# One-hot tables for the gate scatter: the order of VectorE's work in the one-hot part of a streaming-encoder block

## The reference

```
s1, s2  = scores of each token against two sets of 128 keys, per head (8 heads)
i1, i2  = top 16 of each; the best 16 of the 16 x 16 sums give the experts e = e1 * 128 + e2
gates   = softmax(best 16 scores)
a       = einsum("td,thkd->thk", x, u[e])         # dot with the expert's row of u
y       = einsum("thk,thkd->td", gates * gelu(a), v[e])
```

## Time and profile before

| | |
|---|---|
| median of 3 runs | 3572.12 us |
| profiled execution, its own time | 3572.59 us |
| its span | 3570.8 us |
| mean granted clock of TensorE, share of full | 0.95 |
| TensorE busy | 3241.3 us (91%) |
| VectorE busy | 2623.8 us (73%) |
| ScalarE busy | 1100.5 us (31%) |
| GpSimd busy | 653.5 us (18%) |
| moved by DMA | 883.48 MB, mean 247 GB/s |

### The profile page before, as it was taken

One profiled execution on the slowest core, in us unless ns is written; L12 is line 12 of the kernel. 1 busy time (PEld: TensorE's weight loads), 2 busy tenths in 40 slices (PEclk: granted clock), 3 DMA queues, 4 the chain that ended last, 5 costly groups with the idle time before them and its releaser, 6 DMA issues.

```text
span 3570.8 us, 46376 instructions
## 1 busy us (share of the span) xinstructions
PE 3241.3 (91%) x17301; PEld 2956.9 (83%) x17301; DVE 2623.8 (73%) x3074; ACT 1100.5 (31%) x1015; POOL 653.5 (18%) x428
## 2 busy tenths in 40 slices
PE   1598878879979899999999999999999998999999
PEld 0386764537757799999998898889999998999999
DVE  6868986865563388888877777774777777777777
ACT  2123124432122344444323223332333332233332
POOL 0200000000020002222102211220433333233333
PEclk7599989979979999999999999999999999999999
DMA  8572221125524437777647777777999998999997
GB/s 351 218 282 94 85 77 65 74 82 203 203 89 164 155 139 287 277 270 282 236 182 280 276 290 306 285 287 273 353 349 348 343 349 308 359 348 350 342 348 288
DMA packets 241085, 883.48 MB, mean 247 GB/s; under 512 B 17680, under 2 KB 132496, under 8 KB 169744
## 3 DMA queue, kind: packets, MB, share of 16 engines
q1 hardware_dynamic: 161552, 545.82, 41.2%
q0 software_dynamic: 55296, 268.46, 20.0%
q10 hardware_dynamic: 24192, 68.64, 5.1%
HBM read 824.13 MB, written 58.72 MB: 247 GB/s over the span
## 4 chain that ended last, share of the span: by engine, by line
PE 63%; DVE 20%; DMA 6%; issue 5%; ACT 4%; DVEq 1%; SPq 0%; POOL 0%; ACTq 0%; PEldq 0%
PE bank L1595 9%; PE bank L1596 9%; PE bank L1597 9%; PE bank L1294 9%; PE bank L1295 8%; PE bank L1296 8%; DVE u_row L1125 3%; ACT w_hi L430 3%; DVE tap_a L893 2%; DMA w_raw<-wwq 2%; DVE tap_b L893 2%; DMA ada_w<-wada 2%; DVE w_lo L761 2%; PE bank L1486 2%; PE bank L1487 2%
## 5 line engine op out<-in xcount | busy, mean ns | idle before, releaser
L761 DVE TENSOR_TENSOR w_lo<-w_raw,w_hi 128x2048 fp32r<-128x2048 f32 (+1 forms) x327 | 742.5, 2271 | 760.6 <-ACT w_hi L430 748.5
L1294 PE MATMUL bank<-act_hi,w_hi 128*128 128x384 f32 (+1 forms) x2840 | 1034.6, 364 | 177.8 <-POOL act_lo L402 105.6
L430 ACT ACTIVATE w_hi<-w_raw 128x2048 fp32r<-128x2048 f32 (+1 forms) x327 | 621.6, 1901 | 1517.3 <-PE bank L1296 795.8
L1295 PE MATMUL bank<-act_lo,w_hi 128*128 128x384 f32 (+1 forms) x2840 | 1017.7, 358 | 0.0
L1296 PE MATMUL bank<-act_hi,w_lo 128*128 128x384 f32 (+1 forms) x2840 | 1016.6, 358 | 0.0
L1294 PEld LDWEIGHTS bank<-act_hi,w_hi 128*128 128x128 f32 x2840 | 550.1, 194 | 245.9 <-issue 139.5
L1595 PE MATMUL bank<-wt_hi,w_hi 128*128 128x384 f32 x2048 | 688.7, 336 | 17.3 <-DVEq L1255 9.2
L1597 PE MATMUL bank<-wt_hi,w_lo 128*128 128x384 f32 x2048 | 686.7, 335 | 0.0
L1596 PE MATMUL bank<-wt_lo,w_hi 128*128 128x384 f32 x2048 | 686.6, 335 | 0.0
L1296 PEld LDWEIGHTS bank<-act_hi,w_lo 128*128 128x128 f32 x2840 | 549.3, 193 | 34.7
L1295 PEld LDWEIGHTS bank<-act_lo,w_hi 128*128 128x128 f32 x2840 | 551.3, 194 | 30.1 <-issue 0.2
(11 more groups left out here) (232 smaller groups left out, 2596.5 us busy)
## 6 DMA issues: line engine op xcount, KB each, us to landing
w_raw<-u SPq DMA_DIRECT2D x128, 1024.0 KB
w_raw<-v SPq DMA_DIRECT2D x128, 1024.0 KB
ada_w<-wada SPq DMA_DIRECT2D x80, 1024.0 KB, 5.4
gelu_l<-gelu_scratch SPq DMA_DIRECT2D x64, 768.0 KB
gate_l<-gate_scratch SPq DMA_DIRECT2D x64, 768.0 KB
w_raw<-win SPq DMA_DIRECT2D x27, 1024.0 KB
gelu_scratch<-gelu_s ACTq DMA_DIRECT2D x128, 192.0 KB
gate_scratch<-g_chunk ACTq DMA_DIRECT2D x8, 3072.0 KB, 12.4
```

The lines of the kernel that those rows point to most:

```text
L430: act.activation(w_hi[n0 % 2][:, 0:width], w_raw[n0 % 2][:, 0:width], ACT.Copy).then_inc(hi_done, 1)
L761: dve.tensor_tensor(w_lo[s][:, 0:width], w_raw[s][:, 0:width], w_hi[s][:, 0:width].bitcast(F32), ALU.subtract).then_inc(lo_done, 1)
L1294: pe.matmul(out, wh, hi_t(k), start=(k == 0), stop=False)
L1295: pe.matmul(out, wh, lo_t(k), start=False, stop=False)
```

## The change

The five instructions that build a group of one-hots become a function `build_hots(u, i)`. The group for turn 0, u = 0 is built ahead of VectorE's loop. In the loop, which now has 23 turns, VectorE makes the low half of a job, then builds the group that TensorE needs after the job that comes next (u = 1 of the same turn behind the first low half, u = 0 of the following turn behind the second), and takes the dots after that. The 24th turn is written out behind the loop. TensorE's, ScalarE's, GpSimd's and SP's programs are the same.

```diff
-            with dve.Fori(0, 24) as i:
+            def build_hots(u, i):
+
+                dve.wait_ge(hot_used[2 * u + 1], LEAD + i)
+                tok = bass.ds(i * 16 + 8 * u, 8)
+                one = T_.mark(dve.tensor_tensor(hot1[2][:, u], iotas, of_tokens(e1_c, tok), ALU.is_equal))
+                dve.tensor_tensor(hot2[:, u], iotas, of_tokens(e2_c, tok), ALU.is_equal)
+                T_.after(one)
+                for j in range(3):
+                    ins = dve.tensor_tensor(hot1[j][:, u], hot1[2][:, u], of_tokens(gate_c[j], tok), ALU.mult)
+                ins.then_inc(hot_ready[u], 1)
+
+            build_hots(0, 0)
+            with dve.Fori(0, 23) as i:
                 T_.open(i, 2)
                 for u in range(2):
-                    dve.wait_ge(hot_used[2 * u + 1], LEAD + i)
-                    tok = bass.ds(i * 16 + 8 * u, 8)
-                    one = T_.mark(dve.tensor_tensor(hot1[2][:, u], iotas, of_tokens(e1_c, tok), ALU.is_equal))
-                    dve.tensor_tensor(hot2[:, u], iotas, of_tokens(e2_c, tok), ALU.is_equal)
-                    T_.after(one)
-                    for j in range(3):
-                        ins = dve.tensor_tensor(hot1[j][:, u], hot1[2][:, u], of_tokens(gate_c[j], tok), ALU.mult)
-                    ins.then_inc(hot_ready[u], 1)
                     lo(J_U + 74 + u, i)
+                    build_hots(1 - u, i + u)
                     for m in range(1 + u):
                         dot(54 + u + m, i, 3)
-                T_.close(24)
+                T_.close(23)
+            lo(J_U + 120)
+            build_hots(1, 23)
+            dot(123)
+            lo(J_U + 121)
+            for m in range(2):
+                dot(124 + m)
```

## The result

| | median | lowest to highest | runs |
|---|---|---|---|
| before | 3572.03 us | 3570.91 to 3573.41 | 4 |
| after | 3494.23 us | 3492.39 to 3495.50 | 4 |

What follows compares the result with a forecast made beforehand. TensorE was taken to be held up each turn by VectorE's two dots ahead of the u = 0 one-hots. Waits of 52 and clock 25.4 made 77.4 us off 3572.59, about 3495 us, range 3487 to 3517.

Steps and rivals of the forecast that it cites:

- The bound: One-hot part: an 11.9 us chain from the u = 1 job outlasts TensorE's 9.77, making it 2.28 us late each turn.
- The group of u = 0: VectorE's loop: two 2.21 us dots leave the chain; one-hots done at 7.50, slack 2.3 us instead of a 2.28 wait.
- The group of u = 1: VectorE's loop: now behind two dots and the low half, done at 17.27, wanted at 19.54; the moved cost stays hidden.
- The sum: First to last group: 536.62 us becomes 459.2, gaining 77.4: 52 for the waits and 25.4 for the clock.
- The rows' side: Clock in the one-hot part: one of two turns waited without a drop, so the clock term is 25.4, not 37.
- a drop behind each wait: The skill's reading for TensorE's one-hot waits: 23 drops of 1.6 us, giving 52 + 37 = 89.
- The transfers: One-hot part: same bytes in a shorter turn, 331 GB/s instead of 285; rows and loads of u costed at nothing.
- Rival 1: One-hot store turns: late rows or loads stall VectorE's one-hots, 31 us given back in 8 turns, 3526; chance 12%.
- Rivals 2 and 3: One-hot part: 2, transfers at 285 GB/s set pace, 3572, 3%; 3, dots waiting for rows block low halves, 3620, 4%.

Runs made afterwards that it cites:

- The experiment with waits of 1.1 us: Changed kernel with one u = 1 dot and two further, overwritten one-hot instructions ahead of the u = 0 group: 3523.08 us, ratio 0.9863.
- waits are of 3.3 us: Changed kernel with both u = 1 dots and two further, overwritten one-hot instructions ahead of the u = 0 group: 3614.80 us, ratio 1.0118.
- 2 MB a turn more: Changed kernel with 2 MB more copied HBM to HBM on SP's queue in each one-hot turn: 3527.19 us, ratio 0.9873.
- 1 MB more: Changed kernel with 1 MB more copied HBM to HBM on SP's queue in each one-hot turn: 3495.01 us, ratio 0.9785.

## Why the prediction was right

**The bound.** The reading that TensorE is held up in each turn by a chain it starts itself, rounding, low half, two dots, one-hots, is shown from three sides: the dots put back bring back the time, one dot alone costs nothing, and short dots in the old order give the time of the change.

**The group of u = 0.** Forecast from the end of the u = 1 job: low half at 2.15, one-hots from 4.36 to 7.50, wanted at 9.77. In the turn from 2076.54 they stand at 2.14, 4.35 and 7.36 (2078.68, 2080.89, 2083.90), and TensorE takes them at 9.78. The five one-hot instructions take 3.01 us behind a low half, where I had taken 3.14 from behind a dot.

**The group of u = 1.** Forecast: low half at 11.92, one-hots 14.13 to 17.27, dot to 19.48, next low half at 21.7. Found: 11.93, 14.14 to 17.15, to 19.36, 21.70. TensorE takes this group at 19.56, so the slack of 2.3 us is there. (VectorE's idle time of 2.26 us before the last low half is another thing: it is what is left of its own turn.) The runs added that this slack is not used: with the dot in front, which leaves next to none, the time is the same.

**The sum.** 459.2 us from first to last group was forecast, 459.66 measured; 77.4 us of gain, 77.8 measured between the medians. I had split it in 52 for the waits and 25.4 for the clock. That split rested on two turns and a rounded 0.95, and the whole trace of the kernel before bears it out: TensorE takes the group of u = 0 2.26 us late in each of the 23 turns, and seven of the turns last 21.8 us and sixteen 23.4, that is 1.6 more, so 52 and 25. The clock falls behind 16 of 23 waits, never elsewhere in the part. The experiment with waits of 1.1 us supports it: there the lateness alone is paid, 1.22 us a turn for 1.1 shown, and the clock is untouched. The rows' side was the right one to take against a drop behind each wait: that would have given 89. The case on the page (the Trainium skill, TensorE: Matmul & The Clock Gate, "HAM oscillation") has waits of 3 to 5 us, and it was I who carried it over to 2.1. Where the waits are of 3.3 us the trace agrees with it: the clock falls in or behind each of the 23.

**The transfers.** Costed at nothing, and they cost nothing. The share of 0.85 and 330 GB/s are as forecast (0.87 and 331). The room was about as narrow as I had made it out: I gave the loads of u 15.3 us and between 0 and 2.3 us of lateness; behind two of the stores a load took 15.6 us, and the two roundings were late by 0.4. For the rows I counted on a landing of 14.81 us as the worst and 1.3 us to spare; the largest was 14.5, and the closest row landed 2.2 us before its dot. The median of 7.5 that I held against it was that of the faster kind of row, and the second row of u = 1 takes 10.6; this changes no term of the sum. Rival 1, with 12%, asked for a stall in each of 8 store turns; it takes 2 MB a turn more to bring eight such stalls about, and the rows' landing at 15.4 in the median. The mechanism exists, then, and is bound to the stores as I had it, but a dot that waits 1.3 us for its row, as with 1 MB more, still does not reach TensorE: the slack of 2.3 us lies between. By the rule cited for it (the Trainium skill, DMA: Bandwidth & Descriptors, "Issuing engines are not separate DMA queues") the transfers interleave: a copy on SP's queue made the rows of GpSimd's queue slower, 15.4 us for 9.9 with all rows counted in both, so the trace agrees.

**Rivals 2 and 3.** 285 GB/s was no ceiling: the same part ran at 330 and, with more asked of it, at 382 and 403. The loop of dot, issue and landing would have had to pass 22.67 us; with the largest landing of 14.5 it has stayed within 19.56.

## What to carry to other kernels

Where an engine waits once per turn, write down the chain that ends in the wait and the chain that the waiting engine runs meanwhile, both from the same instant. Work that stands in the longer chain without belonging to it can go behind, and it pays until the two are equal; what is moved beyond that is slack, worth having but not worth time. Before counting the gain, add up the bytes of a turn over the shorter turn, since the freed time makes the transfers denser. And when a TensorE wait is priced, look at the granted clock of turns with and without it: the wait's length in the list can be only two thirds of what it costs (here 48.2 of 77 us).

## What the runs showed of the hardware that I had not expected

**The clock does not follow the waits in proportion.** 23 waits of 1.1 us between dense jobs leave the granted clock at 1.00, 23 of 2.1 us bring 0.95, 23 of 3.3 us bring 0.92. Counted in the traces, the clock falls to its lower level behind none of the 23, behind 16, and in or behind all 23. The shortest cost their lateness alone, 28 us; those of 2.1 us cost 52 us by lateness and 25 by the clock; those of 3.3 us 80 and about 40.

**GpSimd's issue of a row takes longer beside some VectorE work than beside other.** GpSimd's timeline in the kernel before, the first two issues of a turn (start us, us), the second running while VectorE builds one-hots in bf16:

```profile
2093.52 2.76 POOL L413 DMA_INDIRECT u_row<-u_rows,urow_i  x1 [10.88 <-DVE u_row L1125]
2096.58 0.94 POOL L413 DMA_INDIRECT u_row<-u_rows,urow_i  x1 [0.30 <-issue]
```

The same in the changed kernel, where the second one begins while VectorE makes a low half in float32:

```profile
2066.90 2.75 POOL L413 DMA_INDIRECT u_row<-u_rows,urow_i  x1 [8.84 <-DVE u_row L1125]
2069.96 2.04 POOL L413 DMA_INDIRECT u_row<-u_rows,urow_i  x1 [0.30 <-issue]
```

0.94 us became 2.04, and 2.75 stays for the first, which in both kernels begins beside a dot in float32. Over the part the second issue takes 0.93 to 0.95 us before and 1.91 to 2.07 after; issues with nothing on VectorE beside them take 0.93 to 0.95 in the changed kernel, so the one-hots beside the second one cost it nothing. It cost nothing here, since no dot of the changed kernel waited for a row, but where indirect transfers are on the path it is a price of moving float32 work next to them. That the type of VectorE's work is the cause, and not another trait of these instructions, was not tried.

**The transfers carried more than any stretch of the kernel had shown as a mean.** With copies from HBM to HBM added, the part held 382 GB/s at a share of 0.95 without a loss, and 403 at 0.98 with one; the 500 us of the part with v have 348 at the same share of 0.95. I did not look into what makes up the difference between the two mixtures.
